# Row-sum reciprocals of the attention stage, made on GpSimd as a power of minus one instead of on VectorE

## What is computed

```python
def _fox_attend(q, cq, qpos, k, v, ck, kpos):
    s = jnp.einsum('bqhd,bkhd->bhqk', q, k, preferred_element_type=jnp.float32) * ATT_SCALE
    ...
    s = jnp.where(mask, s + bias, -jnp.inf)
    p = jax.nn.softmax(s, axis=-1)
    return jnp.einsum('bhqk,bkhd->bqhd', p.astype(v.dtype), v)
```

## Time and profile before

| | us |
|---|---|
| median of 3 executions | 2794.86 |
| lowest and highest of them | 2791.76, 2797.05 |
| the profiled execution, whole | 2794.03 |
| its span (first to last instruction) | 2792.2 |
| busy PE / DVE / ACT / POOL in the span | 2714.9 / 1579.0 / 1005.4 / 210.5 |
| mean granted TensorE clock | 0.991 |

### The profile page before, as it was taken

How to read it: one execution, slowest core, us unless ns; L and a number is a source line. 1 busy time by engine, 2 the same in 40 slices (tenths; PEclk the granted TensorE clock), 3 DMA queues, 4 the chain that set the end, 5 groups by cost and what they waited for, 6 DMA issues and landing times. The chain is left out here.

```text
span 2792.2 us, 47800 instructions
## 1 busy us (share of the span) xinstructions
PE 2714.9 (97%) x18775; PEld 2642.1 (95%) x18775; DVE 1579.0 (57%) x2970; ACT 1005.4 (36%) x2305; POOL 210.5 (8%) x307
## 2 busy tenths in 40 slices
PE   8999989999999999989999999999999999999999
PEld 8999989989999999979999989999999999999999
DVE  6344537556656567548899845464463344434434
ACT  5334336566565666543343422122231111111110
POOL 0000000000000000005565510000000000000000
PEclk9999999999999999999999999999999999999999
DMA  5332353333233343328888854333121111111112
GB/s 177 127 130 79 119 152 111 98 111 117 84 112 108 98 123 107 95 77 197 213 201 207 203 166 138 120 122 136 62 95 47 52 50 45 49 46 46 46 57 98
DMA packets 326657, 308.75 MB, mean 111 GB/s; under 512 B 66529, under 2 KB 283105, under 8 KB 326305
## 3 DMA queue, kind: packets, MB, share of 16 engines
q1 hardware_dynamic: 326432, 305.69, 37.5%
HBM read 218.32 MB, written 87.28 MB: 109 GB/s over the span
## 5 line engine op out<-in xcount | busy, mean ns | idle before, releaser
L512 PE MATMUL banks<-xn_hi,w_hi 128*128 128x352 f32 x1152 | 379.5, 329 | 11.9 <-ACTq L447 7.3
L509 PE MATMUL banks<-w_hi,xn_hi 128*128 128x256 f32 x1376 | 388.9, 287 | 1.0 <-PEq L106 1.0
L509 PE MATMUL banks<-w_lo,xn_hi 128*128 128x256 f32 x1376 | 383.6, 283 | 0.0
L512 PE MATMUL banks<-xn_hi,w_lo 128*128 128x352 f32 x1152 | 379.0, 329 | 0.0
L512 PE MATMUL banks<-xn_lo,w_hi 128*128 128x352 f32 x1152 | 378.7, 329 | 0.0
L509 PE MATMUL banks<-w_hi,xn_lo 128*128 128x256 f32 x1216 | 344.9, 284 | 0.0
L509 PEld LDWEIGHTS banks<-w_hi,xn_hi 128*128 128x128 f32 x1376 | 261.1, 190 | 2.6 <-issue 1.6
L509 PEld LDWEIGHTS banks<-w_lo,xn_hi 128*128 128x128 f32 x1376 | 261.2, 190 | 0.1
L2028 PE MATMUL banks<-mlp_uhi,w_hi 128*128 128x352 f32 x768 | 248.5, 324 | 0.0
L2028 PE MATMUL banks<-mlp_uhi,w_lo 128*128 128x352 f32 x768 | 247.7, 323 | 0.0
L2028 PE MATMUL banks<-mlp_ulo,w_hi 128*128 128x352 f32 x768 | 247.7, 322 | 0.0
(11 more groups left out here) (299 smaller groups left out, 6040.7 us busy)
## 6 DMA issues: line engine op xcount, KB each, us to landing
w_raw<-in_w_in SPq DMA_DIRECT2D x43, 1024.0 KB, 5.7
scratch_xbc<-att_co SPq DMA_DIRECT2D x32, 512.0 KB, 2.8
ssd_ab<-scratch_acum SPq DMA_DIRECT2D x64, 256.0 KB, 5.7
br_g<-scratch_gates SPq DMA_DIRECT2D x72, 176.0 KB, 3.8
w_raw<-in_w_up SPq DMA_DIRECT2D x9, 1024.0 KB, 5.7
scratch_gates<-hand_tanh SPq DMA_DIRECT2D x48, 176.0 KB, 5.2
att_k<-scratch_k_hi SPq DMA_DIRECT2D x64, 128.0 KB
scratch_z<-att_z_stage SPq DMA_DIRECT2D x64, 128.0 KB, 2.0
```

The source lines that it names most:

```text
L509: ins = self.nc.tensor.matmul(self.bank(n, P, PW), x[:, k, t * P:(t + 1) * P], w[:, k, :], start=first, stop=end)
L512: ins = self.nc.tensor.matmul(self.bank(n, P, TT), w[:, k, m * P:(m + 1) * P], x[:, k, r * TT:(r + 1) * TT], start=first, stop=end)
```

## The change

The `invert` steps are taken out of the DVE program in all six places. POOL gets a program in this stage: it sets a column to -1.0 and then runs over all 144 tiles in order, with the waits that `invert` had, and makes `rinv` as `rsum` to the power of that column. The semaphores and their users on ACT are as before.

```diff
+        one, one_set = sb("minus_one", [P, 1]), sem("minus_one_set")
...
+        @block.gpsimd
+        def _(pool):
+            nc.gpsimd.memset(one[:], -1.0).then_inc(one_set, 1)
+            pool.wait_ge(one_set, 1)
+            for e in range(E):
+                m = rows_of(e % ST)
+                pool.wait_ge(s_exp, e + 1)
+                if e >= 2:
+                    pool.wait_ge(p_scaled, e - 1)
+                nc.gpsimd.tensor_tensor(rinv[e % 2][0:m, :], rsum[e % 2][0:m, :], one[0:m, :], ALU.pow).then_inc(inverted, 1)
...
-            def invert(h, s):
-                e, m = h * ST + s, rows_of(s)
-                dve.wait_ge(s_exp, e + 1)
-                if e >= 2:
-                    dve.wait_ge(p_scaled, e - 1)
-                nc.vector.reciprocal(rinv[e % 2][0:m, :], rsum[e % 2][0:m, :]).then_inc(inverted, 1)
...
             top_score(0, 0)
-            invert(0, 0)
             stream.dve(dve, 0, 2, False)
             top_score(0, 1)
-            invert(0, 1)
...
                 tile_ends(h, u, 0)
-                if ngroups[u] <= 2 and nxt:
-                    invert(hn, nxt[0])
                 if early(u) and len(nxt) == 2:
                     top_score(hn, nxt[1])
                 for g in range(2, ngroups[u]):
                     probs_lo(h, u, g)
-                if ngroups[u] > 2:
-                    invert(hn, nxt[0])
-                if early(u) and len(nxt) == 2:
-                    invert(hn, nxt[1])
                 tile_ends(h, u, 1)
                 if not early(u) and len(nxt) == 2:
                     top_score(hn, nxt[1])
-                    invert(hn, nxt[1])
                 add_out(x)
```

## The result

The changed kernel takes 2817.6 us (2816.7 to 2818.3) against 2794.4 us for the kernel before in the same comparison: ratio 1.0087 [1.0074, 1.0099], 23 us slower. The forecast was 2803 with the range 2785 to 2850. The direction and the place were right; the size, +8, was not. The profiled execution is 24.2 us longer than the one before it (2818.28 against 2794.03).

A forecast was written before the change was run, and what follows sets the result against it. PE, with work in 97% of the span, was taken as the bound, the change acting through its waits at units' first turns. Terms +8.8, +1.4, -1.4, -0.7 gave +8.1 on 2794.0; with 0.8 to the median, 2803 us, range 2785 to 2850.

The forecast's parts named there:

- The even tiles: Scale of even tiles on ACT: removing their often late reciprocals from DVE was counted at nothing beyond the relief.
- The handover's outer parts: Around POOL's power: ACT to POOL was taken as 0.08 us, POOL back to ACT as 0.03 us.
- 31 starts without slack: First turns of units starting when scale ends: 16 in unit 3, 9 in unit 2, 5 in unit 1, one in unit 0.
- the sign that I had announced: At unit 3's turn in even heads, PE's wait, none before, was to grow by the handover's excess.
- the excess: Handover from exp to scale in odd tiles: 0.86 us forecast against 0.23 before, so 0.63 us more.
- the other 49: Remaining unit starts, nearly all with 0.5 to 3.8 us of slack, which was assumed not to be needed.
- The term X: Duration of POOL's one-column power, taken as 0.75 us between bounds of 0.10 and 1.42.
- the two cancel: Rival: with X between 0.25 and 0.5 us, about 2794 us, no difference; chance 0.20.
- DVE's relief decides: Rival at units 1 and 2 in odd heads: earlier DVE work removes stalls if X under 0.25; 2786 to 2789 us, 0.20.
- the long routine: Rival: power far longer, say 2.8 us, so all 31 starts pay; 2870 to 2900 us, chance 0.14.
- The relief: DVE, no longer waiting for exps, runs earlier: up to 0.8 us off stalls of units 1 and 2, little in unit 3.
- The third rival: POOL's power blocked by two-input DVE work at about seven unit-1 and unit-2 starts: 4 us more, 2807 us, chance 0.08.

The follow-up runs named there:

- e3_even: Kernel before with only the even tiles' reciprocals made on POOL as powers, the odd ones left on DVE: 2792.5 us, ratio 1.0001.
- e2_held: Changed kernel, but DVE waits at each old place of `invert` until POOL has made the power: 2808.8 us, 1.0061 against the kernel before.
- e5_twice: Changed kernel with a second, unused power on POOL ahead of each one: 2854.2 us, 1.0226 against the kernel before.
- e6_dve_slow: Kernel before with two unused reciprocals on DVE, one after the other, ahead of each one: 2821.6 us, ratio 1.0110.
- e10_memset: Changed kernel with POOL only writing 1.0 into `rinv`, DVE free, rows not normalized: 2783.6 us, 0.9970 against the kernel before.
- e1_mult: Changed kernel with a multiplication in place of POOL's power, rows not normalized: 2796.0 us, 1.0015 against the kernel before.
- e7_mult_held: Changed kernel with multiplication for the power and DVE held as in e2_held, rows not normalized: 2791.4 us, 1.0004 against the kernel before.

## Why the prediction was right in sign and wrong in size

**Right.** PE's waits at the turn were the place. By the distance from one unit's first turn to the next one's (PE's first matmul of each), after is longer than before by 6.3 us ahead of unit 1, 4.8 ahead of unit 2, 10.3 ahead of unit 3 and 0.5 ahead of unit 4. Unit 3 paid 2.1 us in the even heads and 8.2 us in the odd ones. Of the latter 6.6 us are of heads 11, 13 and 15, where a stretch at half clock lies inside the distance. The even tiles cost nothing on balance (e3_even). The handover's outer parts, 0.08 and 0.03 us, were as assumed. The price of a slow reciprocal in this place is shown by e2_held, e5_twice and e6_dve_slow.

**The count of starts.** I counted 31 starts without slack by the weight loads. By PE's own matmuls there were 23: the eight even heads of unit 3 had 0.14 to 0.21 us of cover (the 0.19 to 0.26 named above, less the 0.05 of a start without any). So the sign that I had announced, PE's wait in these heads growing by the excess, shows on the weight loads, which start 0.38 to 0.45 us later, and hardly on PE, whose wait there is 0.06 to 0.13 us. After has 34 such starts by the weight loads (heads 5, 11 and 13 joined in unit 1, so the slack of three of the other 49 was used up), and 34 by the matmuls.

**The term X.** I took 0.75 between 0.10 and 1.42. The plain power takes 0.548 us, so the excess is 0.43 and not 0.63; with it alone changed my sum would have been 14 x 0.43 + 3 x 0.26 - 12 x 0.37 = +2.4 us, hardly a difference. So that my +8 pointed clearly the right way owes something to luck: an X that was too long made up in part for a relief that was too large. X lay just above the 0.25 to 0.5 of "the two cancel", too long for "DVE's relief decides" and far from the long routine. The mean over the 144 is 0.73 us, close to 0.75, but for another reason: 47 of them are over 0.1 us longer than the shortest, beside DVE work (30 beside L1272, 12 beside L1269, 5 others).

**The relief, the step that failed.** I let the stalls of units 1 and 2 win 0.8 us each against the handover's 0.63, so that 12 stalls came out at -2.1 us together. In after the two units cost 6.3 and 4.8 us. The saved wait of DVE (70.9 us in 83 waits for the exp, none now) came back at its next waits for ACT: in front of `add_out` (L2438) 150.6 us instead of 74.4, and in front of the gate step (L1105) 60.4 instead of 35.8. Of the tile that I had traced, tile 5 of head 7, the maximum starts 0.60 us after its scores end where it started 0.69 after, 0.09 us of relief instead of 0.65, and it starts 0.61 after in e2_held, where DVE is not free. What I had not asked is what DVE waits for next. Unit 1's first turn in head 9, where nothing meets, in before, after and e2_held:

```profile
883.99 0.98 PE L2250 MATMUL banks<-ident,att_pr 128*128 128x128 f32 x7 [0.69 <-ACT att_pr L2335]
```

```profile
889.63 0.99 PE L2251 MATMUL banks<-ident,att_pr 128*128 128x128 f32 x7 [1.05 <-ACT att_pr L2336]
```

```profile
890.66 0.98 PE L2251 MATMUL banks<-ident,att_pr 128*128 128x128 f32 x7 [1.05 <-ACT att_pr L2336]
```

Six such starts (unit 1 in heads 3, 9 and 15, unit 2 in heads 6, 9 and 15) pay 0.36 to 0.37 us in after, and as much in e2_held, so the freedom gave them nothing. What it does give lies elsewhere. In after the distances to unit 2 of heads 5 and 7 are 1.2 us shorter each than in e2_held: there PE waited 1.0 us for the exp ahead of the next scores, a wait that was not in my sum, and does not now; part of it was only used up by the late turn of unit 1. Over the whole kernel the move is worth about 6 us to DVE where nothing meets (e10_memset), in units 2 and 3 and less than half of it by the freedom.

**The third rival, which came on top.** I had given "POOL waits for DVE" 0.08 as a case beside the forecast, at +4 us from about seven starts. It is not an alternative but a part of the same case. It has 16 of 64 odd handovers, and eight of them are at starts without slack (unit 1 in heads 1, 5, 7, 11 and 13, unit 2 in heads 1, 11 and 13). There the distance from turn to turn is 0.49 to 0.94 us longer in after than in e2_held, 6.0 us together. With the multiplication it is 5.6 us at the same eight (e1_mult against e7_mult_held). The rule of the Trainium skill ("SBUF — State Buffer", section "Who interferes with whom"), by which a DVE instruction with two SBUF inputs blocks a GpSimd instruction that reads SBUF but not one that only writes it, fits the 34 undisturbed memsets inside L1272 and the 0.78 us of e1_mult in the same place.

**The term that was missing.** Nothing in my sum let a stall cost more than its own length. After has 13.7 us more at half clock in the units, up to 6.8 us lost. In heads 11 and 13 the meeting makes a stall of 1.59 us into 2.16 and 2.17, and the clock falls behind it; in e2_held, without the meeting, it does not, and the distance to the next unit's turn is 1.5 us shorter. At these two turns, then, the stretch at half clock comes with the longer stall; what decides about it in general is not shown here.

**The sum by what was measured.** The plain handover gives +17 (e2_held). The -6 of e10_memset can't simply be added, since part of it is there with DVE held too. After against e2_held shows the rest directly: its units are 7.0 us longer, +6.0 at the eight meetings, +4.4 in units 3 and 4 of heads 11, 13 and 15, where the half-clock stretches differ, and -3.5 in unit 2 of heads 5 and 7 and unit 3 of heads 0, 2 and 4, where the freedom helps. So the meetings cost more than the freedom gave, and the clock came on top. These are distances in one profiled execution each; by the medians, each against before on its own chip, after is 6 us above e2_held.

**Open.** The state-space stage took 4.0 us longer in the profiled execution, with PE's waits for one DMA up from 3.2 to 5.6 us and one more stretch of 3.4 us at half clock. The first stage was 1.9 us shorter. In the experiments the state-space stage took 368.6 to 371.9 us, also with POOL's power in the stage before it (e2_held, e5_twice), so these 4 us don't come from that alone. Their cause stays open.

## What to carry to other kernels

Before a step is moved to another engine, compare its plain duration on the path, not the load that it takes off: here 0.55 us in place of 0.16 on a path that PE waits on at 34 places. An engine that no longer waits gains only up to its next wait, so look for that wait before counting a relief; and look at what the freed engine will then be doing when the moved step wants to start. Count slack on the engine that sets the time: here the weight loads showed less of it than PE's matmuls did. Moving the long operation of the path to the engine that has its input (the scale, to DVE) won 7 us where moving the short one away lost 23.

## What the runs showed of the hardware

- One column of 128 rows on POOL takes 0.098 us as a memset, 0.190 as a multiplication and 0.548 as a power; DVE's reciprocal takes 0.164. By the factor of about two that the Trainium skill names ("GPSIMD Engine Reference", section "Key points") X would have been an estimated 0.33 us; measured against DVE's reciprocal the power has a factor of 3.3, and the trace decides.
- A blocked power ends 0.40 us after the DVE instruction that blocks it (40 of the 47 long ones), a blocked multiplication 0.05 us after. So most of a power's time falls behind the block.
- A memset on POOL, not lengthened inside L1272 in 34 cases, took 0.25 to 0.62 us in 8 cases beside L1269, an operation of one tensor and per-row scalars. I had expected only two-input operations to matter.
- In after the clock went to its lower level behind the stalls of 2.16 and 2.17 us in heads 11 and 13, and did not before at the same turns, with 1.23 and 1.21 us, nor in e1_mult, with 1.82 us in both. A long stall is not always followed by it: at unit 2's turn in head 9 the clock fell at a stall of 2.87 us in before and not at one of 2.77 us in e10_memset.
